# Casting each weight block once: the first tile stores its bf16 blocks to a DRAM scratch, the other tiles reload them on the plain queue

## The chip, the cores and the metric

The kernel runs as one program on all 8 cores of one Trainium2 chip. Every core has one prompt sequence of 2048 tokens and 16 of the 128 sample rows of 4 tokens, and all weights. The metric is device time in microseconds (us) of the slowest core.

## The reference, cut to what matters

Four layers of a decoder trunk. D is 1024, `w_in` is 1024 x 8192 per layer.

```python
def trunk_layer(x, c, h0, buf_a, buf_b, w_c, b_c, w_in, ...):
    mod = jax.nn.silu(c) @ w_c + b_c                       # shift, scale, gate: (B, 3D)
    h = layer_norm(x) * (1.0 + scale) + shift
    a_x, a_z, b_cg, b_bg, b_x, b_z, g_a, g_b = split(h @ w_in)
    xa, new_buf_a = causal_conv(a_x, buf_a, conv_a_w)      # width 4
    hs, h_last = rglru(xa + conv_a_b, h0, w_r, w_i, lam)   # h_t = a_t h_{t-1} + b_t, gates block-diagonal
    o_a = (hs * silu(a_z)) @ w_a_out
    yb, new_buf_b = causal_conv(b_cg * b_x, buf_b, conv_b_w)
    o_b = (b_bg * yb * silu(b_z)) @ w_b_out
    merged = sigmoid(g_a) * o_a + sigmoid(g_b) * o_b
    res = ALPHA * x + gate * (merged @ w_o)
    return layer_norm(res) * ln_g + ln_b, h_last, new_buf_a, new_buf_b
```

All inputs are float32 in HBM. The kernel multiplies in bf16.

## The kernel before, in words

**Tiles and passes.** A core's 2048 tokens are four tiles of 512 tokens. Tiles 0 and 1 go through all four layers together (pass 1, which also carries the 64 sample tokens beside tile 1), then tiles 2 and 3 (pass 2). X, HN, YA, YB and MG stay in SBUF with channels on partitions, so a weight block is the stationary operand and 512 tokens are streamed by it.

**Weight blocks ("units").** Weights lie in HBM as blocks of 128 x 2048 float32 (1 MB). The DMA that loads one casts it to bf16, 128 x 2048, 512 KB in SBUF. There are eight slots WB0 to WB7 for them and one slot WG for the gate block of a layer. A layer has 45 blocks in `wmain`: one gate block, 24 for stage A, 16 for stage B (BA and BB, eight each), 4 for stage P3. `wc` has 12 modulation blocks per layer ("M"), which are used once, by both passes together. A block is 16 matmuls of 512 columns for a prompt tile (16 more of 64 columns for the samples, with tile 1).

**Order of a layer.** For a pair (ta, tb), which is (0, 1) or (2, 3), a list called `plan` holds per layer: the gate block "G"; stage A of ta alone (8 chunks, each three blocks, two gate matmuls, two convolutions, the recurrence); then stage A of tb mixed with stage B of ta, and in pass 1 with the 12 M blocks of the next layer; P3 of ta; stage B of tb mixed with the layer norms of ta; P3 of tb. So every `wmain` block is loaded once per tile, four times in all: 176 blocks x 4 tiles, and the gate block once per pass and layer, 8 times. Below, "A0" is stage A of tile 0, "A1+B0" the mixed stage, and so on.

**What sets the order.** Each operation is recorded with the buffers that it reads and writes, and a list scheduler in the kernel's own Python (`Prog.schedule`, with costs, latencies and one shared "wire" for the transfers written in by hand) sets the order on each engine. The engines run these lists strictly in order, with a semaphore wait ahead of an instruction where it needs one. All weight loads are issued by GpSimd (POOL), in whose list they stand between its elementwise products and small copies; a load waits there until TensorE has read the slot's last block. `ws_pump` keeps up to eight blocks loaded or loading. SP issues 57 rows of other transfers: x tiles, parameters, states, outputs.

**Start.** Tile 0 is loaded by SP straight into the free half of X (`entry`, `X<-xp`, four blocks of 512 KB), normalised there by ScalarE (row statistics on VectorE), transposed by TensorE, and written as HN with the first modulation values. For that the eight blocks M(0, 0..7) have to be multiplied first. POOL issues these eight and the gate block at once.

## Time and profile before

| | us |
|---|---|
| runs | 3142.59, 3157.5, 3376.82; median 3157.5 |
| profiled execution, its own time | 3142.3 |
| span of its slowest core (core 3) | 3140.5 |
| spans of all cores | 3112.2 to 3140.5 |
| TensorE busy | 2865.1 (91%) |
| VectorE busy | 2114.7 (67%) |
| ScalarE busy | 1977.3 (63%) |
| GpSimd busy | 1344.1 (43%) |

The profiled execution is 1.8 us longer than its slowest core's span, and lies at the lower of the two runs that agree; the third run of 3376.82 lies far from both. TensorE's busy time counts overlapping, pipelined matmuls with modelled ends, so it overstates what the engine does; the gaps between stages say more than the share. Stage boundaries in the windows below are the first and last matmuls of a stage on core 3.

### The profile page before, as it was taken

What the parts mean: (1) busy time and instruction counts of PE and PEld (TensorE: products, weight loads), DVE (VectorE), ACT (ScalarE), POOL (GpSimd) and SP (SyncE); (2) the same over time, 40 slices, a digit from 0 to 9 for tenths busy, and PEclk for the clock granted to TensorE, in tenths of its full rate; (3) what the DMA queues carried; (4) which work ended last, traced back from release to release, by engine and by line L of the source; (5) the groups of instructions that cost most, each with busy time, mean ns of one, the idle gap of its engine ahead of it and who ended that gap; (6) DMA issues with size and microseconds to landing.
All of it is one profiled execution on the core that took longest, in us unless ns stands there. A gap on an engine that the chain in (4) does not pass through costs nothing.

```text
span 3140.5 us, 56396 instructions; the slowest of 8 cores (3112.2 to 3140.5 us)
## 1 busy us (share of the span) xinstructions
PE 2865.1 (91%) x16224; PEld 1387.8 (44%) x16224; DVE 2114.7 (67%) x3583; ACT 1977.3 (63%) x3251; POOL 1344.1 (43%) x2158
## 2 busy tenths in 40 slices
PE   3999898899988989899999799998998999999996
PEld 2444454354443544444445344443443444443443
DVE  3766658776578766777756666677666866677564
ACT  3766547676567765587755765567664876467641
POOL 1454424555235543255512444336442554346432
PEclk9999999999999999999999899999999999999998
DMA  9899857699567996577878689867887788777884
GB/s 173 148 175 170 149 89 130 112 168 160 97 117 124 168 158 117 107 135 132 139 139 155 127 171 159 144 115 129 145 149 119 121 142 146 133 125 119 146 155 99
DMA packets 118797, 432.48 MB, mean 138 GB/s; under 512 B 13177, under 2 KB 13305, under 8 KB 118498
## 3 DMA queue, kind: packets, MB, share of 16 engines
q0 software_dynamic: 109440, 398.51, 75.8%
q1 hardware_dynamic: 9058, 30.38, 2.8%
q8 instruction: 139, 2.28, 0.3%
q14 instruction: 160, 1.31, 0.2%
HBM read 816.98 MB, written 10.32 MB: 263 GB/s over the span
## 4 chain that ended last, share of the span: by engine, by line
PE 70%; DVE 8%; DMA 7%; issue 6%; ACT 6%; POOL 2%; DVEq 0%; POOLq 0%; SPq 0%; ACTq 0%
PE PS L522 65%; DMA WB<-wmain 4%; PE PS L776 2%; DVE X L501 2%; PE PS L779 2%; DVE PXA L508 2%; PE PS L529 1%; DMA X<-xp 1%; DMA LT<-xp 1%; ACT L486 1%; ACT PXA L486 1%; POOL PTI L501 1%; DVE PTR L903 1%; DVE LNR L514 0%; ACT X L486 0%
## 5 line engine op out<-in xcount | busy, mean ns | idle before, releaser
L522 PE MATMUL PS<-HN,WB 128*128 128x512 bf16 (+1 forms) x10240 | 1954.3, 346 | 105.6 <-DVE PTZ L508 20.9
L522 PEld LDWEIGHTS PS<-HN,WB 128*128 128x128 bf16 x10240 | 862.7, 99 | 1092.5 <-issue 200.2
L452 POOL DMA_DIRECT2D WB<-wmain x704 | 397.2, 564 | 1141.5 <-PE PS L522 650.1
L486 ACT ACT_TABLE_LOAD x280 | 359.2, 1283 | 133.4 <-PE PS L522 50.9
L508 DVE SCALAR_TENSOR_TENSOR PXA<-PAX,PRM,PXA 128x512 f32<-128x512 f32 x384 | 331.7, 868 | 81.9 <-ACT PXA L486 69.4
L508 DVE SCALAR_TENSOR_TENSOR PTAB<-PTAB,PS 128x512 f32<-128x512 f32 x256 | 174.2, 684 | 218.0 <-PE PS L522 174.5
L486 ACT ACTIVATE PTAB<-PS 128x512 f32<-128x512 f32 x256 | 150.6, 594 | 227.4 <-PE PS L522 206.7
L522 PE MATMUL PS<-YA,WB 128*128 128x512 bf16 (+1 forms) x1280 | 259.0, 346 | 12.2 <-DMA WB<-wmain 7.8
L522 PE MATMUL PS<-YB,WB 128*128 128x512 bf16 (+1 forms) x1280 | 255.3, 343 | 2.9 <-DVE PTAB L508 1.9
L486 ACT ACTIVATE LNR<-X 128x512 fp32r<-128x512 f32 (+1 forms) x272 | 139.5, 534 | 186.8 <-PE PS L779 144.8
L522 PE MATMUL PS<-MG,WB 128*128 128x512 bf16 (+1 forms) x1280 | 239.1, 344 | 11.8 <-DVE MG L501 8.7
L508 DVE SCALAR_TENSOR_TENSOR PBX<-PCB,PRM,PBX 128x512 f32<-128x512 f32 x256 | 211.7, 827 | 28.1 <-ACT PBX L486 22.1
L903 DVE TENSOR_TENSOR_SCAN PTR<-PA,PST,PTI 128x512 f32<-128x512 f32 x128 | 172.7, 1352 | 69.3 <-POOL PTI L501 65.8
L501 POOL TENSOR_TENSOR YA<-PTR,PTZ 128x512 bf16<-128x512 f32 x128 | 178.4, 1394 | 86.0 <-DVE PTR L903 78.4
L501 POOL TENSOR_TENSOR PTI<-PTI,PXA 128x512 f32<-128x512 f32 x128 | 164.1, 1289 | 89.9 <-ACT PXA L486 71.1
L501 POOL TENSOR_TENSOR YB<-PBX,PTBZ 128x512 bf16<-128x512 f32 x128 | 168.5, 1316 | 35.9 <-DVE PTBZ L501 18.9
L522 PEld LDWEIGHTS PS<-YA,WB 128*128 128x128 bf16 x1280 | 109.0, 99 | 136.1 <-issue 23.4
L522 PEld LDWEIGHTS PS<-MG,WB 128*128 128x128 bf16 x1280 | 106.7, 98 | 136.8 <-issue 25.1
L522 PEld LDWEIGHTS PS<-YB,WB 128*128 128x128 bf16 x1280 | 108.7, 98 | 124.1 <-issue 8.8
L514 DVE CAST LNR<-X 128x512 fp32r<-128x512 f32 (+1 forms) x272 | 120.2, 461 | 63.8 <-PE PS L776 58.8
L508 DVE SCALAR_TENSOR_TENSOR X<-PS,MOD,X 128x512 f32<-128x512 f32 x128 | 95.7, 749 | 93.9 <-PE PS L522 89.5
L501 DVE TENSOR_TENSOR PCB<-PS,PBX 128x512 f32<-128x512 f32 x128 | 88.2, 689 | 90.7 <-PE PS L522 57.0
(144 smaller groups left out, 3643.4 us busy)
## 6 DMA issues: line engine op xcount, KB each, us to landing
WB<-wmain POOLq DMA_DIRECT2D x704, 512.0 KB, 7.4
WB<-wc POOLq DMA_DIRECT2D x48, 512.0 KB, 11.9
LT<-xp SPq DMA_DIRECT2D x28, 512.0 KB, 7.1
WG<-wmain POOLq DMA_DIRECT2D x8, 512.0 KB, 11.5
yp<-LT SPq DMA_DIRECT2D x8, 512.0 KB
X<-xp SPq DMA_DIRECT2D x4, 512.0 KB, 32.7
LT<-sst SPq DMA_DIRECT2D x4, 384.0 KB, 7.2
sso<-LT SPq DMA_DIRECT2D x4, 384.0 KB
```

The costliest lines, as they stand in the source:

```text
L452: P.add("pool", lambda e, dst=WB[slot], srcd=seq[j]: e.dma_start(out=dst[:, :], in_=srcd), writes=[WBB[slot]], dma=f"wb{slot}", cost=0.6, ...
L486: return P.add("act", lambda e: e.activation(out=out, in_=in_, func=func, **kw), reads, writes, cost=cost, lat=0.17, tbl=TBL.get(func, 0))
L501: return ew(eng, lambda e: e.tensor_tensor(out=out, in0=in0, in1=in1, op=op), out, [in0, in1], reads, writes)
L508: return ew("dve", lambda e: e.scalar_tensor_tensor(out=out, in0=in0, scalar=scalar, in1=in1, op0=op0, op1=op1), out, [in0, in1], reads, w ...
L514: return ew(eng, lambda e: e.tensor_copy(out=out, in_=in_), out, [in_], reads, writes, rate=0.00104 if in_ps(in_) else 0.00052)
L522: ins = e.matmul(out, l_, r_, start=(i == 0), stop=(i == n - 1))
L529: return P.add("pe", lambda e: e.transpose(out, in_, ident), reads, writes, cost=0.16, lat=0.25)
L776: P.add("pe", lambda e, c=c, xr=xr: e.matmul(ps1, ones, xr, start=(c == 0), stop=(c == NCH - 1)), reads=[LNRB[qx], ONESB], writes=[BANKB[b ...
L779: P.add("pe", lambda e, c=c, sq=sq: e.matmul(ps2, ones, sq, start=(c == 0), stop=(c == NCH - 1)), reads=[LNRB[qs], ONESB], writes=[BANKB[b ...
L903: P.add("dve", lambda e: e.tensor_tensor_scan(out=TR, data0=A, data1=TI, initial=PST[:, l, c, 0:1], op0=ALU.mult, op1=ALU.add), [AB, TIB, ...
```

## The change

Blocks of tile 0 are still loaded and cast by POOL's queue. Behind each of them SP now stores the bf16 block to a DRAM scratch `scr` (180 stores of 512 KB: 176 blocks and 4 gate blocks). Tiles 1, 2 and 3 load their blocks from `scr` on SP's queue without a cast (528 blocks, and 4 gate blocks in pass 2). The M blocks stay on POOL. A slot is free for its next block only when its store has been done as well. A store waits in SP's list for its cast load to land. Besides, the blocks with numbers 2 to 9 of the sequence now read the buffers `XB[c][1]` (tile 0 in the free half of X), so they wait until tile 0 has been normalised.

```diff
-            plan += [("G", l)] + spread([[("A", ta, l, c)] for c in range(NCH)], ex1)
+            plan += [("G", ta, l)] + spread([[("A", ta, l, c)] for c in range(NCH)], ex1)
...
+    scr_d = nc.dram_tensor("scr", [DEPTH * UNITS_PER_LAYER, 128, 2048], BF16, kind="Internal").ap()
+    SCRB = [Buf(f"SCR{i}") for i in range(DEPTH * UNITS_PER_LAYER)]
+    early = [XB[c][1] for c in range(NCH)]
...
+    def load_unit(dst, dstB, key, t, u, reads=()):
+        if t is None or t == 0:
+            srcd = wc_d[u] if t is None else wmain_d[u]
+            P.add("pool", lambda e: e.dma_start(out=dst[:, :], in_=srcd), reads=reads, writes=[dstB],
+                  dma=f"wb{key}", cost=0.6, lat=2.2, xfer=DMA_US)
+            if t == 0:
+                P.add("sp", lambda e: e.dma_start(out=scr_d[u], in_=dst[:, :]), reads=[dstB], writes=[SCRB[u]],
+                      dma=f"ws{key}", cost=0.4, lat=2.2, xfer=1.56)
+        else:
+            P.add("sp", lambda e: e.dma_start(out=dst[:, :], in_=scr_d[u]), reads=[SCRB[u]], writes=[dstB],
+                  dma=f"wh{key}", cost=0.4, lat=2.2, xfer=1.56)
...
-            P.add("pool", lambda e, dst=WB[slot], srcd=seq[j]: e.dma_start(out=dst[:, :], in_=srcd),
-                  writes=[WBB[slot]], dma=f"wb{slot}", cost=0.6, lat=2.2, xfer=DMA_US)
+            load_unit(WB[slot], WBB[slot], slot, *seq[j], reads=early if 2 <= j < 10 else [])
...
-    def gate_weights(l):
-        P.add("pool", lambda e: e.dma_start(out=WG[:, :], in_=wmain_d[l * UNITS_PER_LAYER]), writes=[WGB], dma="wg",
-              cost=0.6, lat=2.2, xfer=DMA_US)
+    def gate_weights(t, l):
+        load_unit(WG, WGB, "g", t, l * UNITS_PER_LAYER)
```

**The start.** POOL's list before: all eight M blocks and the gate block go out at once, then come the first blocks of stage A.

```order
5 L452 DMA WB<-wc 128x2048 x8
6 L978 DMA WG<-wmain 128x2048
7 L708 MEMSET PST 128x192
8 L705 MEMSET ONES 128x128
9 L514 COPY PAX<-PST 128x3 [waits sem_pool]
10 L514 COPY PAX<-PST 128x3
11 L452 DMA WB<-wmain 128x2048 [waits dsem_wb0,sem_pe]
```

POOL's list of the changed kernel at the same place:

```order
5 L451 DMA WB<-wc 128x2048 x2
6 L451 DMA WG<-wmain 128x2048
7 L722 MEMSET PST 128x192
8 L528 COPY PAX<-PST 128x3 [waits sem_pool]
9 L528 COPY PAX<-PST 128x3
10 L719 MEMSET ONES 128x128
11 L451 DMA WB<-wc 128x2048 [waits sem_act]
12 L451 DMA WB<-wc 128x2048 x5
```

Six M blocks now stand behind a wait for ScalarE. SP's list begins with the four `X<-xp` loads in the changed kernel, and has the parameters, the identity and the conditioning vectors behind them; before, these three stood ahead.

**Pass 2, stage A of tile 2, layer 2.** POOL's list before, around chunk 4 (numbers behind WB are slots):

```order
1745 L452 DMA WB2<-wmain 128x2048 [waits dsem_wb2,sem_pe]
1746 L501 TENSOR_TENSOR YB<-PBX,PTBZ 128x512
1747 L514 COPY PST<-PCB 128x2 [waits sem_dve,sem_pool]
1748 L514 COPY PST<-PAX 128x3 [waits sem_act]
1749 L452 DMA WB4<-wmain 128x2048 [waits dsem_wb4,sem_pe]
1750 L501 TENSOR_TENSOR PTI<-PTI,PXA 128x512 [waits sem_act] x2
1751 L452 DMA WB7<-wmain 128x2048 [waits dsem_wb7,sem_pe]
1752 L501 TENSOR_TENSOR YA<-PTR,PTZ 128x512 [waits sem_dve]
1753 L514 COPY PST<-PTR 128x1
```

POOL's list of the changed kernel there:

```order
1364 L528 COPY PST<-PAX 128x3 [waits sem_act,sem_pool]
1365 L515 TENSOR_TENSOR YB<-PBX,PTBZ 128x512 [waits sem_dve]
1366 L515 TENSOR_TENSOR PTI<-PTI,PXA 128x512 [waits sem_act] x2
1367 L515 TENSOR_TENSOR YA<-PTR,PTZ 128x512 [waits sem_dve] x2
1368 L528 COPY PCB<-PST 128x2 [waits sem_pool]
1369 L528 COPY PST<-PTR 128x1
```

The loads, each with its wait for TensorE, have gone from between the products.

**Pass 1, layer 0, start of A1+B0.** SP's list before had nothing of the weights. SP's list of the changed kernel there, stores (`scr<-WB`) and loads (`WB<-scr`) mixed:

```order
53 L457 DMA WB4<-scr 128x2048 [waits dsem_ws0,dsem_wh4,sem_pe]
54 L454 DMA scr<-WB7 128x2048 [waits dsem_wb7]
55 L454 DMA scr<-WB6 128x2048 [waits dsem_wb6]
56 L454 DMA scr<-WB5 128x2048 [waits dsem_wb5]
57 L457 DMA WB1<-scr 128x2048 [waits dsem_ws1,dsem_wb1,sem_pe]
58 L457 DMA WB2<-scr 128x2048 [waits dsem_ws2,dsem_wh2,sem_pe]
59 L457 DMA WB3<-scr 128x2048 [waits dsem_wh3,sem_pe]
60 L454 DMA scr<-WB5 128x2048 [waits dsem_wb5]
```

Three stores, each waiting for a cast load of POOL's queue (`dsem_wb`), stand ahead of three plain loads for tile 1.

## Rows read from the trace of the kernel before

**Rows 1.** The cores: span and mean granted TensorE clock of the slowest.

```profile
core 3: 3140.5 us, clock 0.977
```

**Rows 2.** Windows by stage: A0 of layer 0, A1+B0, P3, B1, next A0, next A1+B0.

```profile
core 3: us, PE busy (x) PEld busy (x) DVE busy (x) ACT busy (x) POOL busy (x), PEclk, DMA share, GB/s
...
64.00:184.00 120.00, 111.01 (x592) 55.84 (x591) 87.88 (x161) 89.08 (x140) 55.41 (x90) 0.97 0.87 159
184.00:360.00 176.00, 163.21 (x1247) 82.72 (x1246) 114.44 (x229) 113.09 (x219) 84.72 (x170) 0.97 0.96 163
360.00:376.00 16.00, 15.49 (x73) 7.42 (x74) 10.53 (x22) 8.75 (x17) 10.15 (x16) 1.00 1.00 163
376.00:471.00 95.00, 90.18 (x628) 47.03 (x627) 56.35 (x107) 46.60 (x83) 20.68 (x27) 1.00 0.54 96
471.00:595.00 124.00, 107.33 (x531) 50.44 (x530) 99.65 (x175) 94.58 (x162) 62.29 (x94) 0.94 0.75 129
595.00:771.00 176.00, 161.75 (x1237) 81.27 (x1235) 124.04 (x261) 121.75 (x229) 95.24 (x180) 0.97 0.91 151
```

**Rows 3.** Windows: A1+B0 of layers 2 and 3 (the last without M blocks).

```profile
1007.00:1177.00 170.00, 156.84 (x1217) 78.44 (x1215) 117.91 (x241) 122.61 (x230) 91.95 (x180) 0.98 0.94 155
...
1410.00:1564.00 154.00, 149.42 (x1032) 73.55 (x1029) 111.06 (x230) 111.05 (x220) 83.67 (x167) 1.00 0.79 132
```

**Rows 4.** Windows, pass 2: A2 of layer 1, A3+B2 of layer 1.

```profile
2058.00:2171.00 113.00, 103.28 (x466) 46.79 (x464) 91.13 (x124) 88.98 (x137) 58.52 (x89) 0.98 0.69 115
2171.00:2310.00 139.00, 134.53 (x624) 60.70 (x622) 88.64 (x114) 90.12 (x128) 66.96 (x109) 1.00 0.87 145
```

**Rows 5.** DMA queues over the whole span: packets, MB, share of the 16 engines.

```profile
q0 software_dynamic: 109440, 398.51, 75.8%
q1 hardware_dynamic: 9058, 30.38, 2.8%
```

**Rows 6.** The same queues between 190 and 290 us.

```profile
q0 software_dynamic: 4462, 16.25, 99.2%
```

**Rows 7.** The last four stores of y, 3111 to 3140.5 us: queue, and one issue with its landing.

```profile
q1 hardware_dynamic: 576, 2.10, 17.6%
...
yp<-PTR SPq DMA_DIRECT2D x1, 512.0 KB, 2.6
```

**Rows 8.** Weight loads as issued, KB each, median us from issue to landing.

```profile
WB<-wmain POOLq DMA_DIRECT2D x704, 512.0 KB, 7.4
```

**Rows 9.** Waits over the span: engine, line, who ended it: us, times, longest.

```profile
PE PS L522 <- DMA WB<-wmain: 27.8, 14, 4.8
...
POOL WB L452 <- PE PS L522: 669.1, 311, 20.8
```

**Rows 10.** Timeline of the start: first and last x block's statistics, normalising, first stage-A matmul.

```profile
25.78 0.69 DVE L569 BATCH_NORM_STATS2 STA<-X 128x6 f32<-128x512 f32 x1 [3.34 <-DMA X<-xp]
...
48.29 1.49 DVE L569 BATCH_NORM_STATS2 STA<-X 128x6 f32<-128x512 f32 x2 [3.71 <-DMA X<-xp]
...
51.02 2.37 ACT L486 ACTIVATE X<-X,RS 128x1024 f32<-128x1024 f32 x2 [0.63 <-DVE RS L508]
...
59.95 0.63 PE L522 MATMUL PS<-SCTb,WB 128*128 128x17 bf16 x16
...
63.67 2.72 PE L522 MATMUL PS<-HN,WB 128*128 128x512 bf16 x6 [1.56 <-DVE STA L569]
```

**Rows 11.** POOL's loads: group over the span (busy, mean ns), waits between 2058 and 2171 us.

```profile
L452 POOL DMA_DIRECT2D WB<-wmain x704 | 397.2, 564 | 1141.5 <-PE PS L522 650.1
...
POOL WB L452 <- PE PS L522: 21.0, 10, 3.1
```

**Rows 12.** The tile PXA, VectorE's convolution step: ns min/median/max; its group's mean.

```profile
L508 DVE SCALAR_TENSOR_TENSOR PXA<-PAX,PRM,PXA x384: 718/750/3405, 69.9 to 2997.4; 128x512 f32<-128x512 f32 x192
...
L508 DVE SCALAR_TENSOR_TENSOR PXA<-PAX,PRM,PXA 128x512 f32<-128x512 f32 x384 | 331.7, 868 | 81.9 <-ACT PXA L486 69.4
```

More of the change, by code:

```diff
@@ L434, in units_of @@
         if k == "M":
-            return [wc_d[at[1] * 12 + at[2]]]
+            return [(None, at[1] * 12 + at[2])]
         if k == "A":
-            o = at[2] * UNITS_PER_LAYER + 1 + 3 * at[3]
-            return [wmain_d[o + i] for i in range(3)]
+            return [(at[1], at[2] * UNITS_PER_LAYER + 1 + 3 * at[3] + i) for i in range(3)]
         if k in ("BA", "BB"):
-            return [wmain_d[at[2] * UNITS_PER_LAYER + 25 + 2 * at[3] + (k == "BB")]]
+            return [(at[1], at[2] * UNITS_PER_LAYER + 25 + 2 * at[3] + (k == "BB"))]
         if k == "P3":
-            return [wmain_d[at[2] * UNITS_PER_LAYER + 41 + at[3]]]
+            return [(at[1], at[2] * UNITS_PER_LAYER + 41 + at[3])]
         return []
+    def load_unit(dst, dstB, key, t, u, reads=()):
[9 more added lines that the diff above has]
+                  dma=f"wh{key}", cost=0.4, lat=2.2, xfer=1.56)
     seq = [u for at in plan for u in units_of(at)]
@@ L991, in _build @@
         elif k == "G":
-            gate_weights(at[1])
+            gate_weights(at[1], at[2])
         elif k == "A":
```

## The prediction

> **What bounds the kernel now.** I read the cores first: core 3 is the slowest, 3140.5 us at a clock of 0.977 [rows 1], and the profiled execution took 3142.3. Then the windows by stage, since the change touches the stages differently. In pass 2 the mixed stage A3+B2 takes 139 us [rows 4] for 40 blocks of 16 matmuls and 16 gate matmuls, 656 in all, 0.212 us each, with hardly a gap: TensorE sets its length. A2 takes 113 us for 400 such matmuls, which would be 85 us; VectorE is busy 91 and ScalarE 89 of them [rows 4]. So stage A alone is a chain over VectorE, ScalarE and POOL, and has about 23 us of TensorE's time to give once its layer-norm matmuls (about 5) are counted. In pass 1 the same stage takes 120 to 124 us [rows 2].
>
> The third view is the DMA share. In A1+B0 of layers 0 to 2 it is 0.96, 0.91 and 0.94 [rows 2, 3]; layer 3, which has no M blocks, has 0.79 and is 22 us shorter than layer 1 (154 against 176). The M blocks explain only 12 x 0.63 = 7.6 us of this on TensorE, 0.63 being the price of one block's 16 small matmuls [rows 10]. The rest, about 14 us, is waiting for weights. The list of waits puts 27.8 us of TensorE's idle time down to weight loads directly [rows 9]; short waits show further in stretched matmul pitches and in what follows. In A0 (0.87 and 0.75) and B1 (0.54) the DMA engines have room.
>
> **Price of a block.** In 190 to 290 us nothing but cast loads runs and the engines are 99.2% busy; 16.25 MB at 0.524 MB a block are 31 blocks, so a cast load costs 99.2 / 31 = 3.2 us of all 16 engines [rows 6]. Over the whole span the same division gives 0.758 x 3140.5 / 760 = 3.13 [rows 5]. The plain queue moved 30.38 MB in 2.8% of the span: 58 blocks' worth in 88 us, 1.5 us each [rows 5]. The four last stores of y, which run alone, cost 0.176 x 29.5 / 4 = 1.3 us each and land 2.6 us after issue [rows 7]. A store of bf16 rows to the scratch is not in the trace; I take 1.5, the price beside other traffic, with 1.3 below and, as the far bound above, the 3.2 of a cast load.
>
> The Trainium skill (DMA: Bandwidth & Descriptors, Anatomy of one DMA) gives a DMA as about 2.0 us fixed plus bytes over 436 GB/s. Counting the float32 source that is 2.4 us of transfer for a cast load and 1.2 for a plain one, 3.6 for load and store against the 4.7 that the rows give; the trace shows the slower figure, 3.2 for a load alone. By the page's figures no stage of tile 0 would come near its limit, and the two positive terms below would be zero.
>
> **The start.** Before, four x blocks share the engines with nine cast loads; the first is used at 25.8 and the last at 48.3, normalising ends at 53.4, and stage A begins at 63.7 [rows 10]. Now only two M blocks and the gate block go beside x: 4 x 1.5 + 3 x 3.2 = 16 us, so x is there by about 17 and normalised by about 23 (5.1 us from the last block to the end of normalising, as before [rows 10]). SP has parameters and conditioning vectors behind x, which are still early enough. Then six M blocks land 3.2 apart after some 4 us: the last at about 23 + 4 + 6 x 3.2 - 3.2 = 43, and stage A begins 3.7 us after the last M block as before [rows 10], at 47 to 50. That is 14 to 17 us earlier, but it is given back. What the engines must move until the last block of A0 is 12 M blocks (38), 25 blocks with stores (25 x 4.7 = 118), x of tiles 0 and 1 in twelve blocks (18) and 3 us of small things: 177 us. With 3 us before the first packet and some 8 us between x's landing and the held-back loads with little to move, and with the last block's matmuls behind, A0 ends at about 191 instead of 184. **Term: +7**, between -10 (stores overlap the loads) and +15.
>
> **A0 of layers 1 to 3.** 25 x 4.7 = 118 us of transfers in stages of 122 to 124 us [rows 2]. It fits, with up to eight blocks loaded ahead in B1, whose share of 0.54 leaves room. A slot is also held until its store lands. I take +2 each, **+6**; at 1.3 a store it is 0, and from 1.7 a store on (123 / 25 - 3.2) each further 0.1 us costs 2.5 us a layer.
>
> **A1+B0.** Before 52 blocks x 3.2 = 166 us of transfers. Now 24 x 1.5 + 16 x 4.7 + 12 x 3.2 = 36 + 75 + 38 = 149. TensorE's own time is that of layer 3 plus the M blocks, 154 + 7.6 = 162 [rows 3]. So TensorE becomes the limit: 176 to 165 in layer 0 (which also loads x), 176 to 164 and 170 to 163 in layers 1 and 2, nothing in layer 3. **Term: -30**, between 0 and -36 (all three stages at 162). P3 of tile 0, 16 us for 4 x 4.7 = 19 us of transfers, begins with blocks loaded ahead: 0, at most +3 a layer. B1 is bound by TensorE and had room: 0.
>
> **POOL.** 532 loads leave its list, 0.564 us each [rows 11], 300 us; and with them the waits for TensorE in that list, 669 us over the span [rows 9], behind which products and copies stand in order. In A2 that was 21 us of waiting [rows 11] and 24 x 0.56 = 14 of issuing in 113 us. Little of it lay on the chain: POOL is busy 58 of 113 us [rows 4], and VectorE and ScalarE stay at 90. Of A2's 23 us of slack I take 5, a fifth, four times; and 2 for each of the four stages with B3 or layer norms whose even chunks POOL multiplies. **Term: -28**, between 0 and -92 (all the slack of four stages). I choose near the small end because the two engines busy for 80% of the stage keep their work.
>
> VectorE's convolution step takes 750 ns in the median but 868 in the mean and up to 3405 [rows 12]: 384 x 0.118 = 45 us of stretch, from whatever it shares with POOL. The Trainium skill (SBUF — State Buffer) says that VectorE and GpSimd share a port pair as an exclusive lock, that a DMA issued from GpSimd needs it to write its descriptors, and that one issued from SP does not. By that rule much of the stretch would go with the 532 issues; the trace shows the stretch but not whose it is.
>
> **Sum.** +7 + 6 - 30 - 28 = -45. From the profiled execution, 3142.3 - 45 = 3097. That execution lies at the low one of the two runs that agree (3142.6 and 3157.5, mean 3150); the median, 3157.5, is the upper one of them. From the mean of the two, 3150 - 45 = **3105**. A measurement of this kernel tells about 2% from no change, 63 us, so this is within it.
>
> **Rivals.**
> - *The relief of POOL is the main effect, faster.* For it: the in-order waits in POOL's list are the largest entries of the list of waits, and VectorE's stretched steps cost time exactly where VectorE is on the chain. If A2 gives up half of its slack (4 x 12), A0 of layers 1 to 3 gains 3 each instead of losing 2, and the stages with layer norms give 12 in all: 7 - 9 - 30 - 48 - 12 = -92, 3058. By the skill's port rule above this is the outcome to expect. Against it: VectorE's and ScalarE's own work of 90 us per A2.
> - *Stores cost what cast loads do, slower.* A write to HBM beside a float32 read stream may cost more than the 1.3 to 1.5 of the rows. At 3.2 a store, A0 has 25 x 6.4 = 160 us of transfers against 123: +37 in three layers, +49 in layer 0, and A1+B0 (36 + 102 + 38 = 176) gains nothing; with -28 from POOL that is +132, 3282. The total turns positive from about 2.1 us a store and passes +2% at about 2.7. Against it: y's stores at 1.3.
> - *SP's list takes back the gain, no change.* A store waits in it for a cast load to land, 7.4 us in the median [rows 8], and plain loads for tile 1 stand behind three such stores. Eight blocks of 3.4 us cover 27 us, so a single wait is hidden, a row of them in A1+B0 may not be. Then the 30 us stay and half of POOL's term: +7 + 6 - 14 = -1, 3149.
> - *The change does not do what it says.* The only place for this is the wait for x, and POOL's list does show it ahead of the third M block; no chance is given to it.
>
> **Chances.** Forecast 0.42, POOL rival 0.28, SP rival 0.20, dear stores 0.10. Faster by over 2% (below 3087 from the base of 3150) is most of the POOL rival, an edge of the forecast and some unforeseen gain: 0.33. Slower by over 2% is most of the store rival: 0.10. The rest, 0.57, is within 2%. The range reaches from just beyond the POOL rival, 3045, to above the SP rival with a store of about 2.2, 3175; it leaves out the dear stores and a full gain of A2's slack.
>
> **What would show it.** DMA: the plain queue moves some 370 MB more, of it 94 MB stores, and the share over the span falls from 0.79 to (228 x 3.2 + 712 x 1.5 + 88) / 3105 = 0.61. Stage A begins near 48 us and A0 ends near 190. The DMA share in A0 rises to 0.9 or more. A1+B0 of layers 0 to 2 take 163 to 165 us. A2 takes 108. I am wrong if a store takes over 1.7 us of the engines, if TensorE waits for `WB<-scr` in A1+B0, or if A2 falls below 103 or stays at 113.

## The result, and the profile after

The change made the kernel 0.7% slower: 3170.6 us in the median of 20 runs (3159.6 to 3593.4) against 3145.1 (3139.0 to 3465.9), a ratio of 1.0071 with an interval of 1.0056 to 1.0086, about +22 us where -45 was forecast. That is under 2%, but the interval lies wholly above 1. The time lies inside the range of the forecast, 3045 to 3175, at its far end; the direction is the wrong one. In some executions of either kernel one die or both show a lower granted clock and the time is 3 to 14% longer; ratios here and below leave these executions out, medians do not, and a run with too few others has a time and no ratio.

The cores of the kernel after, span and mean granted clock of the slowest, and the medians of the two dies:

```profile
core 1: 3171.7 us, clock 0.972
...
die 0 (median of its cores): 3152.2 us, clock 0.974
die 1 (median of its cores): 3149.3 us, clock 0.975
```

No core runs away, so it is the program and not one core; the clock of the slowest core is 0.5% lower than before (0.972 against 0.977 [rows 1]). Now the page's engine table (busy time, share, instructions) and DMA queues (packets, MB, share of the 16 engines):

```profile
PE 2868.1 (90%) x16224; PEld 1390.6 (44%) x16224; DVE 2058.8 (65%) x3583; ACT 1981.1 (62%) x3257; POOL 1057.9 (33%) x1626
...
q0 software_dynamic: 32832, 119.55, 24.2%
q1 hardware_dynamic: 111586, 403.72, 38.0%
```

The change did all it says. The plain queue moves 373 MB more than before [rows 5], and the share of both queues together fell from 0.79 to 0.62 (0.61 was forecast). Over the whole program the transfers became cheaper by a fifth and POOL was relieved, and yet the time rose. So the loss has its place where averages don't look. The windows by stage (length, busy time of each engine with its instructions, granted clock, DMA share, GB/s), for the same stages as in [rows 2 to 4]:

```profile
core 1: us, PE busy (x) PEld busy (x) DVE busy (x) ACT busy (x) POOL busy (x), PEclk, DMA share, GB/s
68.00:226.00 158.00, 118.56 (x599) 57.58 (x600) 89.45 (x158) 87.79 (x137) 53.12 (x87) 0.90 1.02 220
226.00:413.00 187.00, 161.71 (x1241) 82.84 (x1239) 111.41 (x226) 113.83 (x222) 75.49 (x148) 0.95 0.89 197
...
522.00:650.00 128.00, 108.62 (x536) 51.31 (x536) 97.04 (x180) 94.93 (x161) 61.55 (x91) 0.93 1.00 219
650.00:820.00 170.00, 158.84 (x1234) 79.79 (x1233) 118.24 (x257) 120.75 (x231) 78.04 (x155) 0.99 0.90 205
1055.00:1229.00 174.00, 161.91 (x1241) 81.59 (x1242) 122.23 (x258) 119.48 (x230) 79.88 (x158) 0.98 0.90 209
1464.00:1625.00 161.00, 154.72 (x1046) 75.73 (x1044) 114.80 (x238) 113.89 (x223) 70.92 (x145) 0.99 0.73 187
2109.00:2217.00 108.00, 103.53 (x476) 47.48 (x475) 87.91 (x126) 90.62 (x139) 46.88 (x66) 1.00 0.39 127
```

The first row is the finding: A0 of layer 0 takes 158 us instead of 120, with a DMA share of 1.02, which means that the engines are full for the whole of it. Nothing else in the table changed by so much. A1+B0 of layer 0 takes 187 instead of 176 and of layer 1 170 instead of 176. A2 of layer 1 shows 108 instead of 113, but this compares two single cores: on core 3 of the kernel before it is 3 us longer than on the others, and the medians over six cores (see below) are 107.6 before and 108.9 after.

**The start.** The timeline of the kernel after (start, duration or span, engine, what; in brackets the idle time before and who ended it):

```profile
1.06 2.79 SPq L609 DMA_DIRECT2D X<-xp  x4
5.22 0.43 SPq L725 DMA_DIRECT2D LT<-cvec  x1
26.23 1.05 ACT L500 ACTIVATE LNR<-LT 17x1024 fp32r<-17x1024 f32 x1 [20.36 <-DMA LT<-cvec]
33.43 0.20 ACT L500 ACTIVATE RS<-MV 128x2 f32<-128x2 f32 x1
40.27 3.17 POOL L451 DMA_DIRECT2D WB<-wc  x6 [36.08 <-ACT PRM L500]
68.28 6.94 PE L536 MATMUL PS<-HN,WB 128*128 128x512 bf16 x21 [1.53 <-ACT HN L500]
```

x lands at 22.7 us, far earlier than before (its last block was used at 48.3), though 6 us later than the forecast of 17. But ScalarE's first step needs the conditioning vectors, which now stand behind the four x blocks in SP's list and land last. It waits 20.36 us for them, normalising starts at 33.4, the held M blocks are issued at 40.3, and stage A begins at 68.3 and not at 47 to 50. In the first 40 us the engines are busy for 0.58 of the time, and between 20 and 40 us no cast load is under way.

**Where the 31 us between the two profiled spans lie.** By medians over six cores, A0 of layer 0 ends 41.7 us later, pass 1 ends 49.4 later, and pass 2 is 17 us shorter. A second pair of profiles (the first two runs below) gives +42, +16 between the end of A0 and the end of pass 1, and -22 in pass 2. All of the loss is there at the end of the first stage; the rest of pass 1 adds 8 to 16, and pass 2 gives some 20 back.

### The profile page after: what moved, and what is told of

Its sections match the earlier page's. It is cut to its first block, busy times and chain, and to the rows that moved or that the text cites. A ratio compares the mean times of both kernels' runs of the same rounds, so it can differ in the third digit from the quotient of the medians.

```text
span 3171.7 us, 57032 instructions; the slowest of 8 cores (3133.4 to 3171.7 us)
## 1 busy us (share of the span) xinstructions
PE 2868.1 (90%) x16224; PEld 1390.6 (44%) x16224; DVE 2058.8 (65%) x3583; ACT 1981.1 (62%) x3257; POOL 1057.9 (33%) x1626
## 4 chain that ended last, share of the span: by engine, by line
PE 70%; DMA 9%; ACT 7%; DVE 6%; issue 6%; POOL 2%; SPq 0%; POOLq 0%; DVEq 0%; ACTq 0%
PE PS L536 65%; DMA WB<-wmain 4%; DMA WB<-scr 3%; PE PS L790 2%; PE PS L793 2%; ACT L500 2%; DVE PXA L522 1%; PE PS L543 1%; DMA LT<-xp 1%; ACT PXA L500 1%; DVE X L515 1%; POOL PTI L515 1%; DMA WB<-wc 1%; DMA LT<-cvec 1%; DVE PTR L917 1%
## 5 line engine op out<-in xcount | busy, mean ns | idle before, releaser
L522 DVE SCALAR_TENSOR_TENSOR PXA<-PAX,PRM,PXA 128x512 f32<-128x512 f32 x384 | 317.0, 827 | 98.3 <-ACT PXA L500 83.6
L522 DVE SCALAR_TENSOR_TENSOR PBX<-PCB,PRM,PBX 128x512 f32<-128x512 f32 x256 | 202.9, 792 | 32.0 <-ACT PBX L500 25.5
L451 POOL DMA_DIRECT2D WB<-wmain x176 | 99.5, 566 | 323.8 <-PE PS L536 133.7
L515 POOL TENSOR_TENSOR YB<-PBX,PTBZ 128x512 bf16<-128x512 f32 x128 | 171.5, 1340 | 101.8 <-DVE PBX L522 48.3
L528 POOL COPY PST<-PAX 128x3 f32<-128x3 f32 x128 | 34.7, 271 | 456.6 <-ACT PAX L500 447.7
```

The source lines that it names most:

```text
L451: P.add("pool", lambda e: e.dma_start(out=dst[:, :], in_=srcd), reads=reads, writes=[dstB], dma=f"wb{key}", cost=0.6, lat=2.2, xfer=DMA_US)
L515: return ew(eng, lambda e: e.tensor_tensor(out=out, in0=in0, in1=in1, op=op), out, [in0, in1], reads, writes)
L522: return ew("dve", lambda e: e.scalar_tensor_tensor(out=out, in0=in0, scalar=scalar, in1=in1, op0=op0, op1=op1), out, [in0, in1], reads, w ...
L528: return ew(eng, lambda e: e.tensor_copy(out=out, in_=in_), out, [in_], reads, writes, rate=0.00104 if in_ps(in_) else 0.00052)
```

## The experiments

Times are medians of all runs, and ratios, with their 95% intervals, are to the kernel before on the same chip. The chips differ, so times of different runs are compared by their ratios. Stage lengths, of one profiled execution each, are medians over the six cores whose traces hold every matmul, from the last matmul of one stage to that of the next. For most kernels that ran, in us:

```
                      A begins  A0 l0  A1+B0 l0  A0 l1  A1+B0 l1  A0 l2  A1+B0 l2  pass 2
before_again            65.0    121.0   177.3    118.5   179.6    110.6   171.4    1417.0
after_again             68.8    159.5   182.0    125.0   173.7    120.4   175.1    1395.3
vectors_first           63.9    155.8   181.4    125.0   170.0    120.2   174.6    1396.5
no_wait_2               63.9    156.1   172.7    115.5   170.0    111.5   175.6    1394.3
wait_only_2             68.8    121.4   189.4    115.1   170.6    115.2   176.6    1424.2
order_free              64.0    149.6   180.4    133.7   169.3    125.7   168.5    1391.8
tile1_casts_2           68.1    159.9   185.9    120.3   197.7    123.9   187.5    1402.0
cast_layer0_A_2         63.6    120.2   189.0    124.3   164.9    117.0   169.0    1389.5
cast_layer0             63.8    120.5   176.2    128.5   167.1    113.3   168.0    1402.7
order_2p86              63.4    121.4   175.8    120.8   168.1    106.4   170.5    1419.1
order_2p66              64.2    124.1   194.1    115.4   175.9    117.8   171.0    1421.4
```

The last two rows are the kernel before with its lists in another order. They show how far a single stage moves by the order alone: A1+B0 of layer 0 takes 194.1 in one and 175.8 in the other. So one stage's difference below 18 us is not shown to be an edit's own.

### The two kernels again

The kernel before and the kernel after, unchanged, as a measure of repetition.

> The kernel before, unchanged, for its trace on the same chip as the three kernels that follow. Ratio 1.00. Every theory expects stage A of tile 0 in layer 0 to take 120 us and the mixed stage 172 to 176.

Measured: 3154.6 us, 1.0002 (0.998 to 1.0023). The kernel before shows no difference from itself.

> The changed kernel, unchanged, on the same chip. Ratio 1.006 to 1.009; +40 us or so against the kernel before at the end of stage A of tile 0 in layer 0.

Measured: 3188.8 us, 1.0092 (1.0058 to 1.0127), in line with the first 1.0071 (the intervals overlap).

### The wait for x

The wait taken out, the scratch kept:

```diff
-            load_unit(WB[slot], WBB[slot], slot, *seq[j], reads=early if 2 <= j < 10 else [])
+            load_unit(WB[slot], WBB[slot], slot, *seq[j], reads=[])
```

> The changed kernel without the wait for x: all eight M blocks are issued at once again, as before. Theory W (the wait costs the loss of layer 0: the first-stage blocks start 15 us later at the engines): stage A of tile 0 in layer 0 ends at about 200 us instead of 226 and the whole is 20 to 25 us shorter than the changed kernel, ratio to before 0.999. Theory S (the stores make that stage bound by the DMA engines and the wait hardly matters): its end stays at 220 or later and the ratio stays at 1.005 to 1.007.

Measured: 3186.7 us, no ratio. A0 of layer 0 takes 157 us and ends at 222, as theory S has it. Run again:

> The changed kernel without the wait for x, again. If the wait costs the changed kernel anything by itself, the ratio to before is 1.003 or less (changed kernel: 1.007 to 1.009); if stage A of tile 0 in layer 0 is bound by its stores either way, as the traces say (157 us with and without the wait), only the start's 5 us are gained and the ratio is 1.004 to 1.007.

Measured: 3184.8 us, 1.0049 (1.0033 to 1.0066). Against the two comparisons of the kernel after (1.0071 and 1.0092) the wait costs 0.2 to 0.4% (the first of these intervals overlaps with this one), and the scratch the other 0.5%. Stage A begins at 63.9, as before, but A0 still takes 156 us. The windows of the whole stretch up to its end (columns as above), without the wait, on core 2:

```profile
0.00:220.00 220.00, 133.39 (x754) 70.75 (x767) 104.14 (x219) 105.47 (x166) 62.86 (x112) 0.91 0.95 206
```

and with it:

```profile
0.00:226.00 226.00, 133.72 (x775) 69.24 (x776) 109.86 (x221) 107.95 (x169) 63.21 (x112) 0.93 0.94 197
```

Share times length is 209 us of transfers without and 212 with it, so the engines are busy nearly throughout in both. Without the wait stage A begins 5 us earlier and ends 8 us earlier (220 against 228); the other 34 of the 42 us stay.

The wait alone, every tile casting as before and no store (`t == 0` is the condition of the store):

```diff
-        if t is None or t == 0:
+        if True:
...
-            if t == 0:
+            if False:
```

> The kernel before with only the wait of blocks 2 to 9 for x added: no scratch, all tiles cast. Theory W: +15 to +25 us, ratio 1.005 to 1.008, with the DMA engines idle between about 24 and 40 us and the lost time still there at the end of stage A of tile 0. Theory S: stage A of tile 0 has room (share 0.87 before) and catches up, total within +5 us.

Measured: 3218.8 us, no ratio. Again:

> The kernel before with only the wait for x, again. With the engines below their limit in stage A of tile 0, 4 us later at its start are at most kept: ratio 1.000 to 1.002. If the wait costs more than it shows at the start (other order of all lists), ratio 1.004 or more.

Measured: 3197.8 us, 1.0049 (1.0029 to 1.0068), some 15 us. The start is 4 us later than before, as in the kernel after. The rest does not come from there: at the end of pass 1 it stands 2 us behind the kernel before, and pass 2 takes 7 us more (1424 against 1417, A2 of layer 3 121 against 113). What a wait in the first 40 us has to do with pass 2, other than through the order that the scheduler then writes, this run doesn't say.

The wait kept, SP's first instructions in their order of before:

```diff
     est = P.schedule()
+    sp = P.q["sp"]
+    P.q["sp"] = sp[4:7] + sp[:4] + sp[7:]
```

> The changed kernel with the wait for x kept, but parameters, identity and conditioning vectors ahead of x in SP's list, as before. My account of the start: x was there at 23 us, but ScalarE and VectorE stood in their lists behind the conditioning vectors until 26 to 30, and blocks 2 to 9 were issued at 40. With the vectors first they are issued at about 30, stage A begins at 57 to 60 instead of 68, and the end of stage A of tile 0 moves by as much only if the engines are the limit there: 8 to 12 us shorter than the changed kernel. Rival (POOL's refills set that stage, which the model's order fixes): the start moves, the end of the stage by less than 4 us, and the total by less than 5.

Measured: 3174.1 us, 1.0065 (1.0041 to 1.009), against 1.0092 of the kernel after on the same chip. The timeline of this kernel:

```profile
19.24 1.05 ACT L500 ACTIVATE LNR<-LT 17x1024 fp32r<-17x1024 f32 x1 [13.36 <-DMA LT<-cvec]
...
27.03 1.28 ACT L500 ACT_TABLE_LOAD   x1 [6.73 <-DVE MV L585]
...
35.16 3.18 POOL L451 DMA_DIRECT2D WB<-wc  x6 [30.96 <-ACT PRM L500]
```

ScalarE starts 7 us earlier, the held loads go 5 us earlier, stage A begins at 63.9 and A0 ends 8 us earlier. The order of three small loads cost 5 to 8 us in this stage, and the two totals differ by 0.3% with intervals that overlap. The rival on POOL's refills allowed the end less than 4. Normalising still ends at 34.6 us instead of the 23 of the prediction: x is used at 20.5 and not landed at 17, and ScalarE waits 6.73 us more, until 27.0, for VectorE's statistics of it.

### The stores

All tiles cast as before, tile 0's blocks are stored as in the kernel after but never read, no wait:

```diff
-        if t is None or t == 0:
+        if True:
...
-            load_unit(WB[slot], WBB[slot], slot, *seq[j], reads=early if 2 <= j < 10 else [])
+            load_unit(WB[slot], WBB[slot], slot, *seq[j], reads=[])
```

> The kernel before with the 180 stores to the scratch added and nothing else: every tile still casts its own blocks (the scratch is written and never read), no wait for x. Theory S: stage A of tile 0 in layer 0 grows from 120 to 150 us or more, stages A of tile 0 in layers 1 to 3 by 2 to 5, and the mixed stages, now 166 + 24 us of transfers against 162 of TensorE, by 10 to 20 each; total +60 to +90 us, ratio 1.02 to 1.03. Theory W: the stores fit into the room, total below +20, ratio at most 1.006.

Measured: 3318.9 us, no ratio. It differs from no_wait only in that tiles 1 to 3 cast. Over cores 4 to 7 the median span of the profiled executions is 3247 us here and 3140 in no_wait, so the plain loads, with the relief of POOL and the new order, give some 107 us. A0 of layer 0 takes 152 us, and A1+B0 of layer 1 198: in both places the stores come on top of casts.

If A0 of layer 0 is the loss, its blocks should not be stored. They are cast by every tile (as before), all others as in the kernel after, no wait (`u` is the block's number, 0 to 24 are the gate block and stage A of layer 0):

```diff
-        if t is None or t == 0:
+        skip = t is not None and u < 25
+        if t is None or t == 0 or skip:
...
-            if t == 0:
+            if t == 0 and not skip:
```

> The changed kernel without the wait for x, and with the 24 stage-A blocks and the gate block of layer 0 left out of the scheme: all tiles cast these, the other 155 blocks are stored and reloaded as in the change. Theory L (the loss is the stores in stage A of tile 0 in layer 0: they fill the engines and push the refills behind products in POOL's list): that stage ends at 183 to 190 again, 35 us earlier than with the change, the mixed stage of layer 0 grows by up to 15, and the ratio falls to 0.987 to 0.992. Rival (the loss is spread over all of pass 1, layer 0 only shows it first): the gain against the kernel without the wait, ratio 0.996, is below 10 us, ratio above 0.993.

Measured: 3442.6 us, no ratio. Run again:

> The kernel in which all tiles cast layer 0's stage-A blocks, once more, for a ratio from undisturbed runs: 0.988 to 0.992 if the stores beside tile 0's stage A of layer 0 cause the loss.

Measured: 3119.6 us, 0.9921 (0.9906 to 0.9935). It beats both kernels, by 0.8% and 1.5%. Its windows, on core 4:

```profile
64.00:184.00 120.00, 109.89 (x580) 55.84 (x590) 86.78 (x161) 88.99 (x140) 54.07 (x90) 0.97 0.87 157
184.00:374.00 190.00, 164.19 (x1194) 82.49 (x1217) 107.45 (x225) 111.90 (x217) 81.31 (x165) 0.95 1.02 191
```

A0 is back at 120 us with a share of 0.87 and a clock of 0.97 (0.90 in the kernel after, where TensorE idled). But the next stage is now the full one: tile 1 casts its 24 blocks beside tile 0's stores of B0, share 1.02, 190 us. Against no_wait_2 (1.0049) the edit is worth 1.3%, 40 us. A0 of layer 0 gives 36, more than any change of order alone moved a stage; A1+B0 of layer 0 takes 16 back and A0 of layer 1 9, and later stages, each within what the order moves, give the rest.

The same for the stage-A blocks of every layer (`u % UNITS_PER_LAYER < 25`):

> No wait for x; the stage-A blocks of all layers are cast by all tiles, only the B and P3 blocks go by the scratch. If the stores in stages A of tile 0 also cost in layers 1 to 3, these stages return from about 124 to 122 us and the total is at most that of the kernel that does so in layer 0 alone. If the plain loads of stage-A blocks pay (fewer transfers in the mixed stages, fewer issues in POOL's list in pass 2), it is 10 to 40 us slower than that one: mixed stages of layers 1 and 2 at 180 us or more (24 x 3.2 + 16 x 4.8 + 12 x 3.2 = 192 us of transfers), ratio 1.000 to 1.010.

Measured: 3175.8 us, 1.0100 (1.0084 to 1.0117): the second case. A1+B0 of layers 1 and 2 take 194.5 and 187.2 us and pass 2 takes 1414, as before. So storing stage A's blocks pays in layers 1 to 3, by 1.8%, and does not pay in layer 0.

And for all blocks of layer 0 (`u < UNITS_PER_LAYER`), which takes the stores out of the full second stage as well:

> No wait; all 45 blocks of layer 0 are cast by all tiles, layers 1 to 3 go by the scratch. With all tiles casting only the stage-A blocks, the mixed stage of layer 0 has 24 x 3.2 + 16 x 4.8 + 12 x 3.2 = 192 us of transfers and took 189; without its stores it has 166 and should take 173 to 178: 11 to 16 us shorter, less a few us for 20 more casts a tile in pass 2. Ratio 0.987 to 0.990 against 0.992. If that stage isn't bound by its transfers, the ratio stays at 0.992.

Measured: 3145.7 us, 0.9987 (0.9975 to 0.9999). The stage fell from 189 to 176 us, and the total did not follow, it rose by 0.7%: A0 of layer 1 rose from 124 to 128.5, and pass 2 from 1389.5 to 1402.7. A theory on one stage held, the one on the total did not. So a full stage (its share was 1.02) is not yet a reason to leave its blocks out.

### The plain loads of tile 1

Tile 1 casts too, so that A1+B0 has its casts back beside tile 0's stores (wait kept):

```diff
-        if t is None or t == 0:
+        if t is None or t < 2:
```

> The changed kernel, but tile 1 casts its blocks on POOL's queue as before; only pass 2 loads from the scratch. The wait for x stays. It tells what the plain loads of tile 1 give. If plain loads relieved the mixed stages of layers 0 to 2 (my term of -30), this one is 30 us or more slower than the changed kernel, ratio to before 1.016 or more, and its layers 1 and 2 mixed stages take about 176 + 10 us. If the plain loads gain nothing because they wait in SP's list behind stores, it is within 10 us of the changed kernel.

Measured: 3399.2 us over all six runs, three of them at 3248 to 3254; no ratio. Again:

> The changed kernel with tile 1 casting, again. The mixed stages of layers 1 and 2 took 196 and 186 us in its first trace against 169 to 175 in the changed kernel: 38 us, of which some may return in stages A. Ratio 1.017 to 1.021, which prices tile 1's plain loads at 30 us or more. If it is below 1.012, they are worth under 10 us.

Measured: 3244.3 us, 1.0294 (1.027 to 1.0318), 2.0 to 2.2% over the kernel after by its two comparisons. Its A1+B0 of layer 1, on core 1:

```profile
650.00:850.00 200.00, 170.75 (x1248) 83.52 (x1247) 124.27 (x255) 120.07 (x229) 92.74 (x183) 0.94 1.02 184
```

By the table, the stage takes 198 us with casts and stores together, at a full share, 174 with plain loads and 180 before. The plain loads are worth 24 us there, and 18 of these only pay for the stores.

### The order

The scheduler knows a store by three numbers. Here they are near nothing (no wait), so that SP's stores don't push other work back in its model:

```diff
-                      dma=f"ws{key}", cost=0.4, lat=2.2, xfer=1.56)
+                      dma=f"ws{key}", cost=0.05, lat=0.0, xfer=0.0)
```

The reason to try it was a hole in A0 of layer 0 of no_wait_2, where POOL's list reads

```
10 L451 DMA WB<-wmain 128x2048 x8
11 L528 COPY PST<-PAX 128x3
...
17 L515 TENSOR_TENSOR YB<-PBX,PTBZ 128x512
18 L515 TENSOR_TENSOR PTI<-PTI,PXA 128x512
19 L528 COPY PST<-PCB 128x2
20 L515 TENSOR_TENSOR YA<-PTR,PTZ 128x512
21 L451 DMA WB<-wmain 128x2048 x2
```

while before the refill stood behind two copies only. The timeline of no_wait_2 on POOL, and the window in which the engines ran dry:

```profile
86.78 1.62 POOL L515 TENSOR_TENSOR YA<-PTR,PTZ 128x512 bf16<-128x512 f32 x1 [1.89 <-DVE PTR L917]
88.35 1.12 POOL L451 DMA_DIRECT2D WB<-wmain  x2
```

```profile
84.00:92.00 8.00, 7.95 (x38) 3.64 (x38) 7.90 (x10) 4.50 (x8) 5.17 (x11) 1.00 0.50 121
```

> The changed kernel without the wait for x, and with the stores at no cost, latency or transfer in the scheduler's own numbers, so that POOL's list has the refills where the kernel before has them (the first behind two small copies, not behind the products of chunk 0). The stores are all still made. If the late refills caused the loss in stage A of tile 0, layer 0 (engines half idle for 12 us at 84 to 92 us), it ends 10 to 15 us earlier than without the wait, at 207 to 212, and the ratio falls from 0.996 to 0.991 to 0.993. If the sum of the transfers sets it, its end moves by under 5 us, and the ratio stays at 0.995 or above.

Measured: 3183.1 us, 1.0127 (1.0109 to 1.0146). The hole closes, on core 5:

```profile
0.00:215.00 215.00, 127.55 (x735) 68.88 (x736) 99.54 (x211) 101.65 (x161) 58.97 (x108) 0.89 0.95 205
80.00:100.00 20.00, 14.37 (x68) 6.51 (x66) 9.17 (x13) 9.33 (x14) 6.33 (x10) 0.97 1.02 216
```

A0 is 6.5 us shorter, so the late refills are at most a small part of its 36. But A0 of layers 1 and 2 rise by 18 and 14 us, and the total is 0.8% worse than no_wait_2. Which of the changed lists does it is not shown: the longest row of stores in SP's list is 15 here and 13 there. With the same numbers on the best kernel:

> As the kernel in which all tiles cast layer 0's stage-A blocks, with the stores free in the scheduler's numbers too. If the order that the modelled stores give matters beyond layer 0, it is 5 us or more faster than that kernel; if not, the same within 3 us.

Measured: 3168.0 us, 1.0076 (1.006 to 1.0092) against 0.9921: the same edit costs 1.5% there. So between kernels with the scratch, too, the order of the lists alone can move the total by more than the 1.3% above; what speaks for the stores there is the 36 us in the one stage from which they were taken.

How much the order alone does was asked of the kernel before, with `DMA_US`, the modelled time of a cast load, set to 2.86 and 2.66. Nothing but the order changes.

> The kernel before with the scheduler's transfer time of a cast load set to 2.86 us instead of 2.76; the same instructions in other lists. If a new order alone can cost or give about 0.5%, this or its sibling lies 0.2% or more from 1.000 and single stages differ by 5 to 12 us. If order hardly matters, both lie within 0.1%, and the 0.5% of the kernel with the wait alone is the wait's own.

Measured: 3150.7 us, 0.9987 (0.9969 to 1.0005).

> The same with 2.66 us. Same expectation as its sibling: 0.2% or more away from 1.000 in one of the two if the order of the lists alone moves this kernel, both within 0.1% if not.

Measured: 3159.8 us, 1.001 (0.9977 to 1.0044). Stages move by up to 18 us and the totals by nothing that shows. So wait_only_2's 0.5% is not shown to be chance of the order, and it stays open.

## Why the prediction was wrong, by its own steps

Two terms failed, of nearly the same size: the first stage (+7, measured +42) and A1+B0 (-30, measured +7 with layer 3).

**The start, "177 us of transfers", +7: measured +42. This is the step of the sum that failed first.** The picture was right in that the engines are then full, but the sum was too small. Up to the end of A0 they did 0.94 x 226 = 212 us of work; before they did 0.90 x 184 = 166. The two queues from 0 to the end of A0, before and after:

```profile
q0 software_dynamic: 6172, 22.51, 75.7%
q1 hardware_dynamic: 2818, 7.87, 14.1%
...
q0 software_dynamic: 5760, 20.97, 60.9%
q1 hardware_dynamic: 7061, 23.35, 32.6%
```

Three things went wrong.

First, the blocks loaded ahead for the next stage were left out. In this stretch the engines serve also the slots that A1+B0 will use: 20.97 / 0.524 = 40 cast blocks moved where the sum had 37, and four plain loads and two stores of the next stage's blocks, some 20 us in all. The trace of before had it: 37 cast loads, x and small things are 139 us by the prediction's own prices, and the engines did 166; 22.51 / 0.524 = 43 cast blocks moved, six more (19 us), and the plain queue took 26 us where the sum has 21.

Second, the prices were too low. The DMA queues of the kernel after in A0 of layer 0, 68 to 226 us, and its issues (KB each, median us to landing):

```profile
q0 software_dynamic: 4214, 15.30, 63.8%
q1 hardware_dynamic: 5299, 19.29, 37.7%
...
scr<-WB SPq DMA_DIRECT2D x25, 512.0 KB, 17.2
WB<-wmain POOLq DMA_DIRECT2D x18, 512.0 KB, 16.2
```

0.638 x 158 = 101 us for 15.30 / 0.524 = 29.2 blocks is 3.45 us a cast load instead of 3.2, and 0.377 x 158 / 36.8 = 1.62 a plain transfer instead of 1.5. On 37 and 25 blocks that is 12 us, and on x and the small transfers 2. Together they bring 177 to 211 of the 212. The forecast of 191 for the end could thus not have held. The same count applied to the kernel before comes out 27 us short of its 166; it was not made.

Third, the begin of stage A (68 and not 48) failed by the conditioning vectors: "SP has parameters and conditioning vectors behind x, which are still early enough" is the sentence. vectors_first shows that it is worth 5 to 8 us of this stage; no_wait_2 puts all of the wait at 7 to 14 us of the total, with intervals that touch.

What TensorE waits for in the stage, in the list of waits of the kernel after, 68 to 226 us (in total, times, longest):

```profile
PE PS L543 <- ACT LT L500: 19.1, 1, 19.1
PE PS L536 <- DMA WB<-wmain: 10.9, 6, 2.8
PE PS L536 <- DMA WB<-scr: 3.9, 1, 3.9
```

These rows add up to 34 us, nearly all that the stage has grown, and the weights are the smaller part. The first row is tile 1's x, which stands in SP's list behind stores and moves beside them; VectorE and ScalarE get it late, and TensorE, whose list has its transposition next, stands for 19 us while the engines are full:

```profile
109.59 23.08 SPq L454 DMA_DIRECT2D scr<-WB  x7
133.04 0.33 SPq L609 DMA_DIRECT2D LT<-xp  x1
159.95 1.50 DVE L583 BATCH_NORM_STATS2 STA<-LT 128x6 f32<-128x512 f32 x2 [13.70 <-DMA LT<-xp]
164.07 3.71 PE L543 MATMUL PS<-IDN,LT 128*128 128x128 f32 x15 [19.07 <-ACT LT L500]
...
145.00:164.00 19.00, 0.00 (x1) 0.00 (x0) 4.39 (x16) 4.48 (x7) 4.45 (x7) 0.58 1.02 209
```

The granted clock averages 0.58 over this stretch, in which TensorE does nothing, against 1.00 in the 45 us ahead of it. In 226 to 413 us the same stream and the plain loads behind stores stand in the list:

```profile
PE PS L536 <- DMA WB<-scr: 10.4, 3, 8.8
PE PS L543 <- DMA LT<-xp: 9.5, 1, 9.5
```

This is the rival on SP's list. It took A1+B0 of layer 0 (20 us of direct waits) as that rival had it, and tile 1's x in A0 besides, which no case of the prediction had. TensorE's wait for `WB<-scr` in A1+B0 was one of its own signs of being wrong. How much of the 42 us at the start x's place makes beside full engines is not separated by a run. On the slowest core of no_wait_2 TensorE waits 10.7 us for tile 1's x by way of ScalarE and 5.0 for blocks, on that of order_free 2.7 and 1.6, with 17.7 for ScalarE's PXAb instead; A0 takes 156 and 150 us all the same. The waits change place and the length hardly moves, which speaks for the full engines. That the stores cause the stage's growth is shown: it is 152 us with stores and no plain loads (stores_only), 121 with the wait and no stores (wait_only_2), and 120 with this stage's stores taken out (cast_layer0_A_2).

**A0 of layers 1 to 3, +6: measured +18** (6.5, 9.8 and 2.2 in the second pair), in the direction forecast, each within what the order alone moves. The transfers there are nearly as priced. DMA queues of the kernel after in A0 of layer 2, 933 to 1055 us:

```profile
q0 software_dynamic: 3524, 12.85, 66.6%
q1 hardware_dynamic: 4054, 14.78, 34.9%
```

0.666 x 122 / 24.5 = 3.32 us a cast load and 0.349 x 122 / 28.2 = 1.51 a plain one. The stage is full (share 1.01), because the blocks ahead count here too.

**A1+B0, -30: measured about +3 in layers 0 to 2** (+5, -6, +4 in the second pair), with +4 in layer 3. This is the other step that failed. Its DMA work came as computed: 0.90 x 170 = 153 us in layer 1 against the 149 of the prediction. In the same stretch, 650 to 820 us:

```profile
q0 software_dynamic: 4104, 14.97, 55.2%
q1 hardware_dynamic: 5400, 19.70, 33.7%
...
WB<-scr SPq DMA_DIRECT2D x23, 512.0 KB, 8.4
```

3.29 us a cast load, 1.52 a plain one. What failed is the inference that a stage whose transfers take 153 us falls to TensorE's 162. It stays at 170 to 175, with the engines at 0.90 and TensorE at 159 of 170 busy: limited by neither alone. Before, it took 176 to 180 at a share of 0.91, so the share itself hardly changed. A plain load lands 8.4 us after its issue where its transfer is 1.5, and TensorE's longest wait for one in this stretch is 3.5 us. tile1_casts_2 shows that the loads' gain (24 us in layer 1) is real and that the stores use up most of it. In layer 3 the stage grew too, with a share of 0.73. What holds the last 6 to 11 us above 164 was not isolated.

**POOL, -28: measured -17 to -22 in pass 2.** The number is near, and the place was wrong, so that much of it is luck. The prediction took 20 of the 28 from A2, four times 5. By medians over six cores, A2 of the four layers changed by -1, +1, -1 and 0 us in the first pair of profiles and by -3, +1, -1 and 0 in the second. A3+B2 gives 6 in all four layers together, and the stages with B3, the layer norms and P3 give 11 to 13, most of it (6 to 8) in layer 1. cast_all_A shows that this belongs to the loads of pass 2: there stage A's blocks are cast again, A2 of layers 1 to 3 takes 114 to 118 us instead of the 107 to 109 of no_wait_2, pass 2 is back at 1414, and B3 with P3, whose blocks are still plain, keeps its gain. That the loads' place in POOL's list does it, and not the cheaper transfers, is not separated by a run. TensorE's own waits for weight loads in pass 2 are 2.8 us before and 2.0 after, on the slowest core of each, so the transfers do not do it directly. POOL's list of waits and its loads after, against [rows 9] and [rows 11]:

```profile
POOL WB L451 <- PE PS L536: 154.6, 74, 29.7
...
L451 POOL DMA_DIRECT2D WB<-wmain x176 | 99.5, 566 | 323.8 <-PE PS L536 133.7
```

669 us of waiting in that list became 155, all idle time before the loads of `wmain` 324 instead of 1141.5, and pass 2 moved by 20: nearly all of it had cost nothing. The rival that half of A2's slack comes free is refuted.

**The rival of dear stores** is refuted as it was priced: the plain transfers, 25 of 37 blocks of them stores in A0 of layer 0, average 1.62 us of the engines there and 1.51 to 1.52 later, not 3.2, and its outcome of +132 was far off. Slower came out for another reason: in the first stage, where the engines are full, 1.6 us a block and a higher price for the casts beside it lengthen the stage.

**Sum,** by the second pair of profiles: +42, +18, +3 and +4 for A1+B0, -9 for P3 and B1 of pass 1, -22 in pass 2: +36, where the two spans differ by 39 and the medians of the main comparison by 25. Against the forecast of -45 the first stage is off by 35, A1+B0 by 37 with layer 3, the other A0 stages by 12 and POOL by 6; the 9 us that P3 and B1 give were forecast as 0. The first of these is explained but for its split between full engines and the late x, the second only as far as the stores of B0 go.

## What to carry to other kernels

When a change adds transfers to one stage, add up all that the engines move until that stage ends, the blocks loaded ahead for the next stage and the streams of other queues included, and first apply the same count to the kernel before: where it misses the measured share times length, it lacks a term. Look also at what else stands in the list into which the new transfers go (here tile 1's x behind stores).

A cache that is written in the first pass need not hold every block. Here leaving out 25 blocks of layer 0, whose stage had grown by 36 us, took the kernel from +0.5% to -0.8%. But the balance has to be measured stage by stage: the other 20 blocks of layer 0, whose stores stand in a full stage too, are better kept in it (0.7%), and so are the stage-A blocks of layers 1 to 3 (1.8%). Each of these is the total of one order of the lists, and order alone moved such a total by up to 1.5%.

A long in-order wait on an engine off the path is no measure of the gain when it goes, and a term that comes out near its number in another stage than the one it was taken from is not a term that was right.

## What the runs showed of the hardware that was not expected

- A 512 KB store from SBUF lands 2.6 us after issue when alone [rows 7] and 17.2 us after it in A0 of layer 0, though a plain transfer takes only 1.6 us of the engines there. The slot is held all that time (the kernel waits for the store before it loads the slot again). The loads of the other queue take 16.2 us instead of the 7.4 over the span [rows 8], so both wait in line for the same engines. The Trainium skill (DMA: Bandwidth & Descriptors, Issuing engines are not separate DMA queues) says that DMAs of different issuers run on the same 16 engines and interleave; the shares of 63.8% and 37.7%, which add up to 1.02, agree.
- A cast load costs 3.2 us beside others of its kind, 3.29 and 3.32 beside plain traffic in later stages, and 3.45 beside the stores in the first stage. The plain ones cost 1.51 to 1.62. In the Trainium skill (DMA: Bandwidth & Descriptors, Anatomy of one DMA) the two would be estimated at 2.4 and 1.2 us of transfer; these estimates are too low here: the measured prices are a quarter to nearly a half above.
- VectorE's convolution step after, over the span, for [rows 12]: 

```profile
L522 DVE SCALAR_TENSOR_TENSOR PXA<-PAX,PRM,PXA 128x512 f32<-128x512 f32 x384 | 317.0, 827 | 98.3 <-ACT PXA L500 83.6
```

The mean fell from 868 to 827 ns and the longest from 3405 to 2214, with the median at 750, when 532 loads left POOL. The Trainium skill (SBUF — State Buffer, SBUF: two separate sides) says that VectorE and GpSimd share a port pair as an exclusive lock; the direction agrees, but a third of the 45 us of stretch went and not most of it (384 x 0.041 = 16), and A2 became no shorter. No run here separates the port from the changed order of work beside it.
